# A fused two-block transformer layer on one core: the identity first on ScalarE's queue, conditioning ahead of x, small loads and two small products behind the first projection

## The reference

```python
def first_block(x, c, ...):
    cond = jax.nn.silu(c)
    mod = cond @ w_ada[l] + b_ada[l]
    sh1, sc1, g1, sh2, sc2, g2 = jnp.split(mod, 6, axis=-1)
    h = _rms(x, ln1_g[l]) * (1.0 + sc1[:, None, :]) + sh1[:, None, :]
    u = h @ w_in[l]
    fq, fk, fv, fg, dq, dk, dv = jnp.split(u, splits, axis=-1)
    ...
    log_f = jax.nn.log_sigmoid(fg.astype(jnp.float32) + b_f[l].astype(jnp.float32))
    fox_out = _fox_attention(fq, fk, fv, log_f)      # bias: cumulative sum of log_f
    ...                                              # differential attention, w_out, gated MLP
def second_block(x, p, ...):
    ...                                              # spatial gating unit, and
    s_own = s_own + table[:, rel_bucket(dist_own)]   # 16 heads with a relative bias from rel_bias
    ...                                              # MLP, a gate on p, the last norm
```

## Time and profile before

| | us |
|---|---|
| median of 3 runs | 776.28 (776.24 to 776.33) |
| profiled execution, its own time | 775.97 |
| span of its profile | 774.2 |
| TensorE busy | 762.9 |
| VectorE busy | 469.9 |
| ScalarE busy | 394.4 |
| GpSimd busy | 64.9 |

### The profile page before, as it was taken

One profiled execution on the slowest core, in us unless ns is written; L12 is line 12 of the kernel. 1 busy time (PEld: TensorE's weight loads), 2 busy tenths in 40 slices (PEclk: granted clock), 3 DMA queues, 4 the chain that ended last, 5 costly groups with the idle time before them and its releaser, 6 DMA issues.

```text
span 774.2 us, 10494 instructions
## 1 busy us (share of the span) xinstructions
PE 762.9 (99%) x4067; PEld 618.4 (80%) x4067; DVE 469.9 (61%) x617; ACT 394.4 (51%) x563; POOL 64.9 (8%) x84
## 2 busy tenths in 40 slices
PE   8999999999999999999999999999999999999996
PEld 6768766878888898888788877777898888888885
DVE  4567675687766554536684435447568777445454
ACT  2557877564344343535534456666456454425253
POOL 3114121010000000002450000000000000000001
PEclk9999999999999999999999999999999999999999
DMA  9999478838675467457487635325476555655501
GB/s 292 335 355 353 164 299 324 302 115 313 231 237 198 127 223 254 162 195 255 153 297 246 211 110 171 127 83 169 129 214 181 179 208 172 202 179 168 185 27 55
DMA packets 91024, 158.71 MB, mean 205 GB/s; under 512 B 3319, under 2 KB 34259, under 8 KB 89952
## 3 DMA queue, kind: packets, MB, share of 16 engines
q1 hardware_dynamic: 88336, 151.04, 58.1%
q0 software_dynamic: 2352, 6.91, 2.7%
q10 hardware_dynamic: 288, 0.10, 0.1%
HBM read 156.95 MB, written 1.08 MB: 204 GB/s over the span
## 4 chain that ended last, share of the span: by engine, by line
PE 97%; DVE 1%; DMA 1%; ACT 1%; issue 0%; POOLq 0%; ACTq 0%; POOL 0%; DVEq 0%
PE PS L1091 24%; PE PS L1093 23%; PE PS L1092 23%; PE PS L1103 6%; PE PS L1104 3%; PE PS L1346 2%; PE PS L1154 2%; PE PS L1306 2%; PE PS L1375 1%; PE PS L1401 1%; PE PS L1211 1%; PE PS L1248 1%; PE PS L1113 1%; PE PS L1112 1%; PE PS L1114 1%; PE PS L1331 1%
## 5 line engine op out<-in xcount | busy, mean ns | idle before, releaser
L1753 DVE TENSOR_TENSOR wlo<-raw,whi 128x2048 fp32r<-128x2048 f32 (+1 forms) x115 | 264.4, 2302 | 146.7 <-ACT whi L1493 128.9
L1493 ACT ACTIVATE whi<-raw 128x2048 fp32r<-128x2048 f32 (+3 forms) x123 | 225.0, 1829 | 154.7 <-PE PS L1093 151.1
L1091 PE MATMUL PS<-whi,hT 128*128 128x512 f32 (+1 forms) x568 | 223.0, 393 | 1.2 <-DVE hT L1929 0.7
L1093 PE MATMUL PS<-whi,hT 128*128 128x512 f32 (+1 forms) x568 | 216.7, 382 | 0.0
L1092 PE MATMUL PS<-wlo,hT 128*128 128x512 f32 (+1 forms) x568 | 216.4, 381 | 0.0
L1091 PEld LDWEIGHTS PS<-whi,hT 128*128 128x128 f32 x568 | 106.8, 188 | 25.5 <-issue 5.9
L1093 PEld LDWEIGHTS PS<-whi,hT 128*128 128x128 f32 x568 | 106.8, 188 | 21.1
L1092 PEld LDWEIGHTS PS<-wlo,hT 128*128 128x128 f32 x568 | 107.0, 188 | 18.2
L1091 PE MATMUL PS<-whi,hidT 128*128 128x512 f32 x216 | 84.4, 391 | 0.0
L1093 PE MATMUL PS<-whi,hidT 128*128 128x512 f32 x216 | 84.1, 389 | 0.0
L1092 PE MATMUL PS<-wlo,hidT 128*128 128x512 f32 x216 | 84.1, 389 | 0.0
(11 more groups left out here) (280 smaller groups left out, 832.8 us busy)
## 6 DMA issues: line engine op xcount, KB each, us to landing
raw<-in_w_in SPq DMA_DIRECT2D x34, 1024.0 KB, 5.1
raw<-in_w_ff SPq DMA_DIRECT2D x32, 1024.0 KB, 5.3
raw<-in_w_ada SPq DMA_DIRECT2D x16, 1024.0 KB, 5.5
raw<-in_w_gate SPq DMA_DIRECT2D x10, 1024.0 KB, 5.8
raw<-in_w_up SPq DMA_DIRECT2D x10, 1024.0 KB, 5.0
raw<-in_w_down SPq DMA_DIRECT2D x10, 1024.0 KB, 4.8
raw<-in_w_ada SPq DMA_DIRECT2D x16, 512.0 KB, 8.1
raw<-in_w_out SPq DMA_DIRECT2D x8, 1024.0 KB, 5.3
```

The source lines that it names most:

```text
L1091: pe.matmul(o, ah, wh, start=(k == 0), stop=False)
L1093: return pe.matmul(o, al, wh, start=False, stop=end)
L1493: act.activation(split_view(whi, i)[:, c], slab_view(raw, slot, i)[:, c], ACT.Copy).then_inc(hi_made if i else part_whi, 1)
L1753: dve.tensor_tensor(split_view(wlo, i)[:, c], slab_view(raw, slot, i)[:, c], whole(split_view(whi, i))[:, c], ALU.subtract).then_inc(lo_ma ...
```

## The change

On ScalarE's queue the identity is issued before c, and the five loads of small vectors that stood behind are gone from it. GpSimd's five loads at its start, and its four (lamb, hot, table, mask) behind the fourth step, go with them to one place behind the seventh step (`part_lo` 7); the two loads of b_f stay behind the fourth step, with a semaphore of their own. "cond" is turned before x. Of the idle products, cond's one is gone and root0 has one in place of five. The fourth of VectorE's multiplies of x becomes a step "xn3" behind the first slab's "wlo". "vectors" and "relbias" move from the steps for j = 5 and 6 to behind "logf", on TensorE, VectorE and GpSimd; ScalarE's heads 0 waits for `col_made`.

```diff
-    order += [("sums0", 0), ("xT", 0), ("cond", 0), ("chunk", 0), ("norm", 0), ("root0", 0), ("rows", 0), ("early", 0),
-              *early, ("col", 0), ("part0", 0), ("wlo", 0), ("rest", 0)]
+    order += [("cond", 0), ("sums0", 0), ("xT", 0), ("chunk", 0), ("norm", 0), ("root0", 0), ("rows", 0), ("early", 0),
+              *early, ("col", 0), ("part0", 0), ("wlo", 0), ("xn3", 0), ("rest", 0)]
...
-            order += {KC - 2: [("relbias", 0)], KC - 3: [("vectors", 0)]}.get(j, [])
...
-    order += [("fgate", 0), ("unit", 0), ("unit", 1), ("logf", 0)] + early
+    order += [("fgate", 0), ("unit", 0), ("unit", 1), ("logf", 0), ("vectors", 0), ("relbias", 0)] + early
...
-split:8 split:9 EV:fox0 fgate:0 EV:fox1 split:10 unit:0 unit:1 logf:0 split:11 scores:0 scores:1 probs:0
+split:8 split:9 EV:fox0 fgate:0 EV:fox1 split:10 unit:0 unit:1 logf:0 vectors:0 relbias:0 split:11 scores:0
...
-                    pe.wait_ge(cond_in, 32)
                     pe.wait_ge(x_in, 16)
...
-                    idle_work(5)
+                    idle_work(1)
...
                 elif kind == "cond":
+                    pe.wait_ge(cond_in, 32)
                     pe.transpose(PS[:, 5, 0:KC], crow[:, :], ident[0:KC, 0:KC]).then_inc(c_ps, 1)
                     reader[5] = [(c_col, 1)]
-                    idle_work(1)
...
+            act.dma_start(con[:, C_ID:C_ID + P], A["constants"][:, C_ID:C_ID + P]).then_inc(cond_in, 16)
             act.dma_start(crow[:, :], A["c"].rearrange("a (r q) -> (a r) q", q=P)).then_inc(cond_in, 16)
-            act.dma_start(con[:, C_ID:C_ID + P], A["constants"][:, C_ID:C_ID + P]).then_inc(cond_in, 16)
...
-            for name, v in (("ln2_g", V_LN2), ("norm_mix_g_2", V_MIX), ("norm_ffn_g_2", V_FFN), ("norm_ple_g_2", V_PLE)):
-                act.dma_start(vec[v:v + KC, :], A[name].rearrange("a (r q) -> (a r) q", q=P)).then_inc(vec_in, 16)
-            act.dma_start(vec[V_BS:V_BS + KC, :], A["b_sgu_spatial_2"][0]).then_inc(vec_in, 16)
...
+                    if u == 0:
+                        act.wait_ge(col_made, 1)
...
-                    for b in range(4):
+                    for b in range(3):
...
+                elif kind == "xn3":
+
+                    dve.wait_ge(xT_ps, 4)
+                    dve.tensor_tensor(xn1[:, :, :].rearrange("p t d -> p (t d)")[:, 3 * W:4 * W].rearrange(
...
+                    dve.wait_ge(bf_in, 32)
...
-                    pool.dma_start(lamb[:, :, :], A["diff_lam"].to_broadcast([P, 4, HD])).then_inc(setup_in, 16)
+                    for r in (0, HD):
+                        pool.dma_start(bf[r:r + FOX, :], A["b_f"].rearrange("a h -> h a")).then_inc(bf_in, 16)
+
+                elif kind == "part0" and i == KC - 2:
+                    pool.wait_ge(part_lo, KC - 1)
+                    for name, v in (("ln2_g", V_LN2), ("norm_mix_g_2", V_MIX), ("norm_ffn_g_2", V_FFN), ("norm_ple_g_2", V_PLE)):
+                        pool.dma_start(vec[v:v + KC, :], A[name].rearrange("a (r q) -> (a r) q", q=P)).then_inc(vec_in, 16)
+                    pool.dma_start(vec[V_BS:V_BS + KC, :], A["b_sgu_spatial_2"][0]).then_inc(vec_in, 16)
+                    for name, r in (("fox_qk_g", V_QK), ("diff_qk_g", V_QK + 2)):
+                        for h in range(2):
+                            pool.dma_start(vec[r:r + 2, h * HD:(h + 1) * HD], A[name][0]).then_inc(qk_in, 16)
...
```

More of the change, by code:

```diff
@@ L382 @@
 DVE_ORDER = written("""
-split:8 split:9 EV:fox0 fgate:0 EV:fox1 split:10 unit:0 unit:1 logf:0 split:11 scores:0 scores:1 probs:0
[L384 to L401, removed]
+split:8 split:9 EV:fox0 fgate:0 EV:fox1 split:10 unit:0 unit:1 logf:0 vectors:0 relbias:0 split:11 scores:0
+scores:1 probs:0 split:12 EV:diff0 lam:0 scores:2 probs:1 values:0 split:13 probs:2 EV:diff1 unit:2 scores:3
@@ new lines @@
+unit:3 values:1 split:14 probs:3 scores:4 values:2 split:15 probs:4 scores:5 probs:5 values:3 ada:15
+scores:6 split:16 probs:6 scores:7 diffnorm:0 probs:7 split:17 turn:diff.0.0 diffnorm:1 mod:1 ada:19
+turn:diff.0.1 pT:0 split:18 psplit:0 EV:w_out0 mod:2 EV:w_out1 gained:norm.1.0 gained:norm.1.1
+gained:norm.1.2 part:norm.1.0 part:norm.1.1 split:19 part:norm.1.2 gained:norm.1.3 part:norm.1.3 split:20
+split:21 split:22 gate2:0 EV:gate0 split:23 EV:up0 split:24 turn:hid.0.0 turn:hid.0.1 split:25 gate2:1
@@ new lines @@
+EV:gate1 split:26 split:27 EV:up1 split:28 turn:hid.1.0 turn:hid.1.1 split:29 gate2:2 EV:gate2 split:30
+split:31 EV:up2 split:32 turn:hid.2.0 turn:hid.2.1 split:33 gate2:3 EV:gate3 split:34 split:35 EV:up3
+split:36 turn:hid.3.0 turn:hid.3.1 split:37 EV:gate4 split:38 split:39 EV:up4 gate2sum:0 split:40
+turn:hid.4.0 turn:hid.4.1 split:41 EV:gate5 split:42 split:43 EV:up5 split:44 turn:hid.5.0 split:45 split:46
+split:47 split:48 split:49 EV:down0 split:50 split:51 turn:norm.2.0 turn:norm.2.1 split:52 split:53 split:54
@@ new lines @@
+split:55 EV:down1 split:56 turn:norm.2.2 turn:norm.2.3 split:57 split:58 split:59 layernorm:0 split:60
+split:61 split:62 split:63 split:64 split:65 split:66 split:67 sgu:0 split:68 split:69 split:70 split:71
+sgu:1 split:72 scores:8 split:73 probs:8 scores:9 split:74 split:75 scores:10 back:8 split:76 split:77
+scores:11 probs:9 back:9 probs:10 back:10 scores:12 probs:11 split:78 split:79 back:11 probs:12 scores:13
+back:12 probs:13 scores:14 split:80 scores:15 back:13 EV:ga0 split:81 merge:0 probs:14 split:82 back:14
@@ L402 @@
+turn:merge.0.0 probs:15 turn:merge.0.1 split:83 EV:ga1 split:84 back:15 merge:1 turn:merge.1.0
+turn:merge.1.1 split:85 EV:w_out20 split:86 turn:norm.3.0 turn:norm.3.1 split:87
 """)
@@ L614, in build @@
         setup_in = sem("setup_in")
+        bf_in = sem("bf_in")
         late_bias_in = sem("late_bias_in")
@@ L932, in squares_of @@
             return hid1[:, 0, t, :] if n in (1, 2) else fin[:, t, h * W:(h + 1) * W]
-        NSETUP = 6
+        NSETUP = 4
         QB = ((0, P), (P, 3 * P))
@@ L1889, in _ @@
                                           twice(aff1[:, 1, :]), ALU.mult).then_inc(xn_made, 1)
+                elif kind == "xn3":
+                    dve.wait_ge(xT_ps, 4)
+                    dve.tensor_tensor(xn1[:, :, :].rearrange("p t d -> p (t d)")[:, 3 * W:4 * W].rearrange(
+                        "p (j s) -> p j s", j=2), PS[:, 3, :].rearrange("p (j s) -> p j s", j=2),
+                                      twice(aff1[:, 1, :]), ALU.mult).then_inc(xn_made, 1)
                 elif kind == "sums" and i == (5, 0):
@@ L2223, in _ @@
                 pool.wait_ge(zeroed, 2 + part)
[L2225 to L2228, removed]
             for it in ORDER:
@@ L2258, in _ @@
                     pool.wait_ge(part_lo, 4)
-                    pool.dma_start(lamb[:, :, :], A["diff_lam"].to_broadcast([P, 4, HD])).then_inc(setup_in, 16)
+                    for r in (0, HD):
[8 more added lines that the diff above has]
+                            pool.dma_start(vec[r:r + 2, h * HD:(h + 1) * HD], A[name][0]).then_inc(qk_in, 16)
+                    pool.dma_start(vec[V_DN:V_DN + 1, :], A["diff_norm_g"]).then_inc(qk_in, 16)
                     pool.dma_start(hot[:, :], A["constants"][0:BUCKETS + 1, C_HOT:C_ALL]).then_inc(setup_in, 16)
                     pool.dma_start(table[0:BUCKETS, :], A["rel_bias_2"]).then_inc(setup_in, 16)
-                    for r in (0, HD):
-                        pool.dma_start(bf[r:r + FOX, :], A["b_f"].rearrange("a h -> h a")).then_inc(setup_in, 16)
                     pool.dma_start(con[:, C_MASK:C_ALIBI], A["constants"][:, C_MASK:C_ALIBI]).then_inc(setup_in, 16)
+                    pool.dma_start(lamb[:, :, :], A["diff_lam"].to_broadcast([P, 4, HD])).then_inc(setup_in, 16)
                 elif kind == "norm":
```

## The result

The changed kernel takes 787.73 us (787.37 to 788.16, 4 runs) against 776.29, 1.46% more: ratio 1.0146, interval 1.0134 to 1.0158. The profiled execution took 787.51 with a span of 785.7, 11.5 above the kernel before in both. The forecast was 788.6, range 785.3 to 791.0.

A forecast was written before the change was run, and what follows sets the result against it. TensorE, busy 99% of the span, was taken as the bound, so any new wait is paid in full. Terms 8.8 + 2.3 + 1.2 = 12.3; 775.97 + 12.3 + 0.31 = 788.6 us, range 785.3 to 791.0.

The forecast's parts named there:

- The wait for bank 6: Behind fgate, relbias waits for the scan's cum_made with diff0 queued behind it: +8.8 us (8.0 to 9.3).
- The clock: After TensorE's wait, its first products run at the slow clock: about +2.3 us, bounds 0 and 4.1.
- skew at scores 1: Skew's transfer lands late, delaying VectorE's scores 0 and TensorE's scores 1: +1.2 us, bounds 0 and 1.5.
- The sum: Whole kernel: 8.8 + 2.3 + 1.2 = 12.3 us of loss, giving 788.6 us; main case 60 in 100.
- the wait alone: Rival: the clock doesn't fall and skew lands early, leaving 8.8 us of loss, 785.4 us; 13 in 100.
- The early edits: At the start, TensorE reaches its first real product 1.3 us earlier (0 to 3.1), swallowed by the later wait.
- the faster rival: At relbias, cum_made is already there, so only the early gain is left: 775.0 us, at most down to 773.2; 4 in 100.
- The moved loads: Fourteen small loads behind the seventh step: last lands near 61, lateness hidden; rival that they delay slab 9, 789.5 us, 10 in 100.
- No time given back: Behind scores 1 nothing is changed and TensorE is the bound, so none of the loss is recovered.

The follow-up runs named there:

- d: Changed kernel with fgate's reader of bank 6 named as fg_abs (VectorE's first instruction of fgate) in place of cum_made (the scan): 775.91 us, ratio 0.9992.
- b: Kernel before with only vectors and relbias moved behind fgate; loads, identity, cond and idle products as before: 788.54 us, ratio 1.0156.
- c: Changed kernel with 20 idle products put behind fgate's, into TensorE's wait: 785.07 us, ratio 1.0112.
- k: Changed kernel with relbias in bank 7 (no wait for bank 6), vectors and relbias right behind fgate, hot and table on their own semaphore: 775.10 us, ratio 0.9983.
- a: Kernel before with identity first, cond ahead of x, fewer idle products and xn3; small loads, vectors and relbias left in place: 776.09 us, ratio 0.9998.
- h: d with cond behind x again and the five idle products back: 775.12 us, ratio 0.9987.
- m: k with cond behind x again and the five idle products back: 775.42 us, ratio 0.9989.

## Why the prediction was right, step by step

**The wait for bank 6, +8.8.** Right in mechanism and nearly in size. Forecast: TensorE idle from 62.2 to 72.3; measured: 62.55 to 72.11. Without the clock's part in relbias (1.44 us, where 0.74 is usual), diff0 would start at 72.11 + 0.74 = 72.85, 8.6 after 64.27. d shows that it is this semaphore, b that it needs nothing else of the change. TensorE paid the wait in full: none of it came back later. That VectorE's chain hangs on slab 9's landing and not on TensorE held: 14.90 us against 14.92.

**The clock, +2.3.** Right in mechanism, too small: 11.5 - 8.6 = 2.9 by the trace, 2.7 by c. I had taken the loss of the first block of idle products; the slow stretch behind the wait, 72.11 to about 77.7, was longer than that block, and half of its 5.6 us is 2.8. The size had come from an analogy with the program's start. I had read the slow pace there as 1.2 GHz, but in the kernel before the granted clock is 1.00 over 0 to 10 us, through the slow products too; so the record of the clock doesn't bear that reading out, and it rests on the pace alone. Behind the wait both show it, the pace and the granted clock. The trace agrees with the Trainium skill (TensorE: Matmul & The Clock Gate, "HAM oscillation — how this bites in real kernels") that a long wait for data costs the fast clock, with 0.50 granted in 72.10 to 77.50.

**skew at scores 1, +1.2.** Wrong: it cost nothing. The step that failed is "it lands 4.7 after", the value near the upper bound taken from the only row of skew, which stood in a saturated stretch (share 1.05). Behind the wait the stream was nearly dry (share 0.22 and 0.09), and skew landed in 1.8 us, ahead of scores 0 at 88.60. The long wait is not needed for that: in d, without it, skew met a share of 0.25 in 74 to 76 us and took 1.8 us as well, while in k, at a share of 1.00, it took 6.1. The lower bound had been named, under 3 us for no loss, and was the right value.

**The sum.** 8.6 + 2.9 + 0 = 11.5 measured against 8.8 + 2.3 + 1.2 = 12.3: two of the errors, 0.6 too little for the clock and 1.2 too much for skew, had opposite signs, so that the sum came out 0.8 off is in part luck. The lower end of the range was also misadded: the wait alone is 776.28 + 8.8 = 785.1, not 785.4, and so lay just outside the stated 785.3; nothing hung on it.

**The early edits.** That their lead never enters the time was right, but I had it at 1.3 us at the first product and only swallowed by the wait. It was 2.0 (16.77 before, 14.81 after), and it came from elsewhere. The identity's 0.64 gave nothing, as TensorE then stood 0.85 us for c and began at 6.73, where it had begun at 6.82. The idle products, which I had called "cover, not path", were on the path: the first product of w_ada, right behind them, started at 11.16 in place of 13.44. Run a shows that this lead would have been lost without the wait too, to the weight stream. The forecast of the faster rival, 775.0, would have been wrong for that reason: with the early edits alone the time is 776.1, and with the whole change and no wait, in d, 775.9.

**The moved loads.** Hidden, as forecast, and no delay of slab 9 came of them: it landed 0.8 earlier, more than the 0.5 forecast. I had given that lead to the early edits; a (58.07) and h (57.16) show that it comes with the moved loads. b, which has the two products moved but not the loads, has it not (58.22). It is the one gain that reached the changed kernel's time: it fits the 0.8 us by which b is slower. My landing of the last one near 61 was early; d measured 63.1. In the changed kernel it lay under the wait.

**No time given back.** Right: three marks and the end are all 11.5 late.

## What to carry to other kernels

When an instruction moves past another that uses the same buffer, look up what the buffer's reader is in the new order: a semaphore that was good enough when nobody waited for it (here the scan's, 9 us after the last read) becomes the price, and naming the true last reader gave all of it back. A lead gained ahead of a saturated stream was worth nothing at its end here; price it by the landing of the slab that the chain hangs on. And take a transfer's time from a stretch with the load that it will meet: the same 24 KB took 1.8 us at a DMA share of 0.10 to 0.25, and 4.7 and 6.1 at 1.05 and 1.00.

## What the runs showed of the hardware that I had not expected

The moment at which TensorE's products pass from the slow to the fast pace at the program's start differs between kernels that begin alike. x's 16 transposes took 1.97 us in the changed kernel, some 0.11 each, and 3.68 in a_early_only, whose first instructions are the same but for the small loads.

```profile
6.88 1.97 PE L1175 MATMUL PS<-con,x 128*128 128x128 f32 x16
```

```profile
6.61 3.68 PE L1175 MATMUL PS<-con,x 128*128 128x128 f32 x16
```

The small loads are not needed for the difference: h and m begin with the same instructions, those loads included, and their transposes took 1.97 and 3.67 us. The granted clock reads 1.00 at both paces, so the record of the clock doesn't show the change. In the changed kernel and in a it cost nothing, since root0 waits in the one for the roots (1.5 us) and the stream takes the rest. What decides between the two paces was not tried.
